# Half of the second-half weight sums of down made ahead in attention, with moved loads and reordered ends, in a one-core encoder layer

## What is computed

```python
def forgetting_attention(h, w_in, b_f, g_q, g_k, w_out):
    proj = jnp.einsum('bsd,de->bse', h, w_in)
    q = rmsnorm(q, g_q)
    k = rmsnorm(k, g_k)
    log_f = jax.nn.log_sigmoid((f_logit + b_f).astype(jnp.float32))
    c = jnp.cumsum(log_f, axis=1).transpose(0, 2, 1)
    ...
        s = jnp.einsum('bqhd,bkhd->bhqk', qb, k).astype(jnp.float32) * scale
        s = s + (cb[..., :, None] - c[..., None, :])
        p = jax.nn.softmax(s, axis=-1).astype(v.dtype)
    ...
    return jnp.einsum('bsd,de->bse', o, w_out)

def swiglu(h, w_gu, w_down):
    gu = jnp.einsum('bsd,df->bsf', h, w_gu)
    gate, up = gu[..., :D_FF], gu[..., D_FF:]
    return jnp.einsum('bsf,fd->bsd', jax.nn.silu(gate) * up, w_down)
```

## Time and profile before

| | us |
|---|---|
| median of 3 runs (2125.92 to 2126.33) | 2126.15 |
| the profiled execution | 2126.24 |
| its span, first to last instruction | 2124.3 |
| PE busy | 2109.8 (99%) |
| DVE busy | 1524.6 (72%) |
| ACT busy | 943.3 (44%) |
| POOL busy | 192.8 (9%) |

### The profile page before, as it was taken

One profiled execution on the slowest core, in us unless ns is written; L12 is line 12 of the kernel. 1 busy time (PEld: TensorE's weight loads), 2 busy tenths in 40 slices (PEclk: granted clock), 3 DMA queues, 4 the chain that ended last, 5 costly groups with the idle time before them and its releaser, 6 DMA issues.

```text
span 2124.3 us, 28271 instructions
## 1 busy us (share of the span) xinstructions
PE 2109.8 (99%) x10402; PEld 1846.7 (87%) x10402; DVE 1524.6 (72%) x2106; ACT 943.3 (44%) x1279; POOL 192.8 (9%) x355
## 2 busy tenths in 40 slices
PE   9999999999999999999999999999999999999998
PEld 8999999999998888888888888888888788887886
DVE  4565566565455435888888888987988977969978
ACT  6333333333344325444444444444544554554533
POOL 0332332233221000000000000000000000000000
PEclk9999999999999999999999999999999999999999
DMA  6465656665243334666666666666666887867866
GB/s 187 118 190 185 211 186 189 198 197 178 80 123 139 119 119 144 203 206 194 226 220 198 219 211 212 209 222 212 198 232 226 276 277 240 266 220 259 266 193 208
DMA packets 269052, 422.45 MB, mean 199 GB/s; under 512 B 17010, under 2 KB 116372, under 8 KB 265636
## 3 DMA queue, kind: packets, MB, share of 16 engines
q1 hardware_dynamic: 248336, 354.77, 52.9%
q10 hardware_dynamic: 20628, 66.49, 8.8%
HBM read 369.52 MB, written 51.68 MB: 198 GB/s over the span
## 4 chain that ended last, share of the span: by engine, by line
PE 96%; DVE 2%; DMA 1%; issue 0%; SPq 0%; ACTq 0%; DVEq 0%
PE gemm L596 11%; PE gemm L597 11%; PE gemm L598 11%; PE gemm L800 11%; PE gemm L802 11%; PE gemm L801 11%; PE aux L800 8%; PE aux L802 8%; PE aux L801 8%; PE aux L597 1%; PE aux L598 1%; PE aux L596 1%; PE aux L851 1%; PE aux L650 1%; DVE f_lo L1475 1%; PE aux L622 0%
## 5 line engine op out<-in xcount | busy, mean ns | idle before, releaser
L1475 DVE TENSOR_TENSOR f_lo<-f_raw,f_hi 128x1536 fp32r<-128x1536 f32 (+1 forms) x230 | 455.0, 1983 | 73.6 <-ACT f_hi L1133 41.3
L596 PE MATMUL gemm<-w_hi,act_t 128*128 128x384 f32 (+2 forms) x1280 | 450.7, 352 | 0.0
L597 PE MATMUL gemm<-w_lo,act_t 128*128 128x384 f32 (+2 forms) x1280 | 443.9, 347 | 0.0
L598 PE MATMUL gemm<-w_hi,act_t 128*128 128x384 f32 (+2 forms) x1280 | 443.9, 347 | 0.0
L800 PE MATMUL gemm<-f_hi,a_form 128*128 128x512 f32 x1056 | 411.1, 389 | 0.0
L802 PE MATMUL gemm<-f_hi,a_form 128*128 128x512 f32 x1056 | 411.0, 389 | 0.0
L801 PE MATMUL gemm<-f_lo,a_form 128*128 128x512 f32 x1056 | 410.8, 389 | 0.0
L800 PE MATMUL aux<-f_hi,a_form 128*128 128x512 f32 x792 | 311.8, 394 | 3.1 <-DVE f_lo L1475 2.5
L802 PE MATMUL aux<-f_hi,a_form 128*128 128x512 f32 x792 | 308.4, 389 | 0.0
L801 PE MATMUL aux<-f_lo,a_form 128*128 128x512 f32 x792 | 308.4, 389 | 0.0
L1089 ACT ACTIVATE f_hi<-f_raw 128x1536 fp32r<-128x1536 f32 x132 | 196.3, 1487 | 214.6 <-DMA f_raw<-in_ffn_w_gate_up 78.7
(11 more groups left out here) (188 smaller groups left out, 2255.3 us busy)
## 6 DMA issues: line engine op xcount, KB each, us to landing
f_raw<-in_ffn_w_gate_up SPq DMA_DIRECT2D x264, 512.0 KB, 4.2
w_raw<-in_fox_w_in SPq DMA_DIRECT2D x189, 256.0 KB, 3.5
f_raw<-in_ffn_w_down SPq DMA_DIRECT2D x88, 512.0 KB, 4.6
f_raw<-in_ffn_w_gate_up SPq DMA_DIRECT2D x88, 256.0 KB, 4.0
f_raw<-t_scratch SPq DMA_DIRECT2D x44, 512.0 KB, 4.8
w_raw<-in_fox_w_out SPq DMA_DIRECT2D x16, 1024.0 KB, 5.1
pre_w<-in_ffn_w_down ACTq DMA_DIRECT2D x22, 512.0 KB, 5.3
pre_rows<-in_ffn_w_down ACTq DMA_DIRECT2D x22, 512.0 KB, 7.1
```

The costliest lines, as they stand in the source:

```text
L596: mm(out, a_hi, b_hi, start=first, stop=False)
L597: mm(out, a_hi, b_lo, start=False, stop=False)
L598: return mm(out, a_lo, b_hi, start=False, stop=last)
L1475: v.tensor_tensor(f_lo[:, n % 4, 0:3 + g], f_raw[:, n % 4, 0:3 + g], f32(f_hi[:, n % 3, 0:3 + g]), ALU.subtract).then_inc(f_lo_done, 1)
```

## The change

Three sets of sums a head in place of two. The third is the second column half (`col = u // 2 * CW`) of the even steps; it is loaded in slot 10 into the first set's buffer, once the first set's store has landed, added on DVE in slot 13 and stored in slot 15. Rounds 12, 14 and 16 (odd `r - R_DOWN`) thereby find ready sums for 4, 4 and 3 of their 8, 7 and 7 steps, and skip L1520 to L1527 for these. Most entries of the `LOADS` tables move by one or two units. At the start the transposes of the second half of x's first column block move behind PE's first six real matmuls, 8 filling matmuls become 6, and ACT issues three small loads (`load_wf`) after its first weight split. At the end the last two stores of block 3 go to ACT's queue.

```diff
+    def early_sums(r, j):
+        if r < R_DOWN:
+            return False
+        return (r - R_DOWN) % 2 == 0 or (FIRST[(r - R_DOWN) // 2] + j) % 2 == 0
...
-    dram_t = nc.dram_tensor("t_scratch", (PRE_END, 2, P, 4, CW), F32, kind="Internal").ap()
+    dram_t = nc.dram_tensor("t_scratch", (PRE_END, 3, P, 4, CW), F32, kind="Internal").ap()
...
-        LOADS_1 = [(0, 0, 0, 4), (0, 1, 1, 6), (0, 2, 4, 10), (0, 3, 7, 13), (0, 4, 8, 14), (0, 5, 8, 14), (0, 6, 11, 17), (1, 0, 9, 14), (1, 1, 12, 18), (1, 2, 13, 19), (1, 3, 14, 19), (1, 4, 14, 20), (1, 5, 16, 20), (1, 6, 17, 23)]
+        LOADS_1 = [(0, 0, 0, 5), (0, 1, 1, 6), (0, 2, 5, 11), (0, 3, 7, 12), (0, 4, 10, 14), (0, 5, 8, 13), (0, 6, 11, 17), (1, 0, 9, 14), (1, 1, 12, 18), (1, 2, 13, 20), (1, 3, 14, 18), (1, 4, 14, 19), (1, 5, 14, 19), (1, 6, 17, 26)]
...
-                    made = dram_t[PRE_FIRST + step // 2, step % 2]
+                    made = dram_t[PRE_FIRST + step // 2, step % 2 if (r - R_DOWN) % 2 == 0 else 2]
...
-            sp.wait_ge(c22_out[0], 1)
-            sp.dma_start(y_cols[3][:, 2], rows[:, 3, 2]).then_inc(y_stored, 16)
...
-            sp.wait_ge(c22_out[1], 1)
-            sp.dma_start(y_cols[3][:, 3], rows[:, 3, 3]).then_inc(y_stored, 16)
...
                         rows_slot(G[t], 0, 0, t, True, False, width, ks=(2 * half, 2 * half + 1))
+                        if half == 0 and t == 0:
+                            pe.wait_ge(x_ld[0], 16)
+                            transpose_rows(0, 0, (2, 3))
...
-            keep_warm(5)
-            pe.wait_ge(x_ld[0], 16)
-            transpose_rows(0, 0, (2, 3))
-            keep_warm(3)
+            keep_warm(6)
...
             def load_blocks(h, u):
-                act.wait_ge(pre_stored[u], 16 * (h - PRE_FIRST) + 16)
-                src = w_down_v[bass.ds(h - PRE_FIRST, 1), u].rearrange("o p r c x -> (o p) r c x")
+                if u == 1:
+                    act.wait_ge(pre_stored[1], 16 * (h - PRE_FIRST) + 16)
+                else:
+                    act.wait_ge(pre_stored[0], 32 * (h - PRE_FIRST) + 8 * u + 16)
+                src = w_down_v[bass.ds(h - PRE_FIRST, 1), u % 2].rearrange("o p r c x -> (o p) r c x")
+                col = u // 2 * CW
...
                     if sums and s in (8, 13):
                         store_sums(h, {8: 0, 13: 1}[s])
+                    if sums and s == 10:
+                        load_blocks(h, 2)
...
                     if s >= 13:
                         evac(h, s - 13)
+                    if sums and s == 15:
+                        store_sums(h, 2)
...
+            for t in range(2):
+                act.wait_ge(c22_out[t], 1)
+                act.dma_start(y_cols[3][:, 2 + t], rows[:, 3, 2 + t]).then_inc(y_stored, 16)
...
                     if s >= 13:
                         evac(h, s - 13)
+                    if sums and s == 13:
+                        pre_sums(h, 2)
                     if s >= 14:
                         normalise_qk(h, s - 14)
...
-                sums = n + 2 < NU and UNITS[n + 2][1] == 1 and not summed_early(UNITS[n + 2][0])
+                sums = n + 2 < NU and UNITS[n + 2][1] == 1 and not summed_early(n + 2)
```

More of the change, by code:

```diff
@@ L85, in encoder_layer @@
         his += 1 + g_
-        ts += g_ and (r_ < R_DOWN or (r_ - R_DOWN) % 2 == 1)
+        ts += g_ and not early_sums(r_, j_)
         HI_COUNT.append(his)
@@ L332, in encoder_layer, with summed_early @@
         assert len(SPLIT_NTH) == 2 * NSTEP
-        def summed_early(r):
-            return r >= R_DOWN and (r - R_DOWN) % 2 == 0
+        def summed_early(n):
+            return early_sums(UNITS[n][0], UNITS[n][2])
         w_down_v = w_down.rearrange("(g r i p) (c x) -> g i p r c x", r=2, i=2, p=P, c=2)
@@ L432, in _ @@
                     sp.dma_start(f_raw[:, s, 2], src[:, 1, 1, col:col + CW]).then_inc(f_ld[s], 16)
-                elif not summed_early(r):
+                elif not summed_early(n):
                     for half in range(2):
@@ L438, in _ @@
                     if r == R_DOWN and j == 0:
-                        for b in range(2):
-                            sp.wait_ge(pre_stored[b], 16 + 8 * NSTEP)
-                    made = dram_t[PRE_FIRST + step // 2, step % 2]
+                        sp.wait_ge(pre_stored[0], 16 + 16 * NSTEP)
+                        sp.wait_ge(pre_stored[1], 16 + 8 * NSTEP)
+                    made = dram_t[PRE_FIRST + step // 2, step % 2 if (r - R_DOWN) % 2 == 0 else 2]
                     for half in range(2):
@@ L913, in _ @@
             act.dma_start(b_f_all[:], b_f.broadcast_to((P, NH))).then_inc(bf_ld, 16)
-            for kg in range(1, KG):
-                load_wf(kg)
             def transposed_hi(n, kg, i):
@@ L976, in load_blocks @@
             def load_blocks(h, u):
[L977 to L978 removed]
+                if u == 1:
[4 more added lines that the diff above has]
+                col = u // 2 * CW
                 for r in range(2):
[L980 removed]
+                    act.dma_start(pre[u % 2][:, 2 * r:2 * r + 2], src[:, r, :, col:col + CW])\
+                        .then_inc(pre_ld[u % 2], 16)
             def store_sums(h, u):
[L983 removed]
+                act.wait_ge(pre_step, 9 * (h - PRE_FIRST) + 3 * u + 3)
                 dst = dram_t[bass.ds(h, 1), u].rearrange("o p f x -> (o p) f x")
[L985 removed]
+                act.dma_start(dst, pre[u % 2][:]).then_inc(pre_stored[u % 2], 16)
             def in_chunk(h, second=False, last=False, sums=False):
@@ L1034, in _ @@
                 split_hi(0, 0, half, in_proj=True, first=True)
+                if half == 0:
+                    for kg in range(1, KG):
+                        load_wf(kg)
             for kg in range(KG):
@@ L1060, in form_read @@
                 act.wait_ge(xform_tr, 2 * q + 1)
+                if q == 0:
+                    act.wait_ge(pre_stored[0], 16 + 16 * NSTEP)
                 if 0 < q < 6:
@@ L1090, in weights_hi @@
                 else:
-                    if not summed_early(r):
+                    if not summed_early(n):
                         act.wait_ge(t_step, 3 * T_COUNT[n] + 1)
@@ L1130, in weights_hi_rest @@
             def weights_hi_rest(n):
-                if not summed_early(UNITS[n][0]):
+                if not summed_early(n):
                     act.wait_ge(t_step, 3 * T_COUNT[n] + 3)
@@ L1375, in pre_sums @@
             def pre_sums(h, u):
-                f = pre[u]
-                dve.wait_ge(pre_ld[u], 32 * (h - PRE_FIRST) + 32)
+                f = pre[u % 2]
+                if u == 1:
+                    dve.wait_ge(pre_ld[1], 32 * (h - PRE_FIRST) + 32)
+                else:
+                    dve.wait_ge(pre_ld[0], 64 * (h - PRE_FIRST) + 16 * u + 32)
                 on_its_own(dve)
                 v.tensor_tensor(f[:, 0:2], f[:, 0:2], f[:, 1:4:2], ALU.add).then_inc(pre_step, 1)
-                dve.wait_ge(pre_step, 6 * (h - PRE_FIRST) + 3 * u + 1)
+                dve.wait_ge(pre_step, 9 * (h - PRE_FIRST) + 3 * u + 1)
                 on_its_own(dve)
                 v.tensor_tensor(f[:, 3], f[:, 0], f[:, 3], ALU.add).then_inc(pre_step, 1)
-                dve.wait_ge(pre_step, 6 * (h - PRE_FIRST) + 3 * u + 2)
+                dve.wait_ge(pre_step, 9 * (h - PRE_FIRST) + 3 * u + 2)
                 on_its_own(dve)
```

4 lines of the change are left out of this document (2 added, 2 removed).

## The result

The changed kernel takes 2129.45 us (median of 13 runs, 2128.24 to 2131.74), the kernel before 2125.92 us (13 runs, 2122.05 to 2127.51). The ratio is 1.0017 with a 95% interval of 1.0010 to 1.0024: 3.5 us more, just under the 0.2% that the prediction called "slower". Forecast were 5.3 us more.

What follows compares the result with a forecast made beforehand. PE, busy 2109.8 of 2124.3 us, was taken to bound the kernel. Profiled 2126.24 + 10.7 (attention) - 4.9 (down) - 0.1 (start) - 0.4 (end) = 2131.5, 2131.4 as median; range for 8 in 10: 2120.3 to 2136.0.

Steps and rivals of the forecast that it cites:

- The chain in attention: Attention, heads 2 to 12: third set's additions behind tile 0's readout delay tile 3's norm; 0.97 us a head, 10.7 us.
- rival A: Attention hides the third set, PE never waits for tile 3's norm: 2120.7 us, ends 2120 and 2124; chance 0.2.
- the stop of 0.2 us at tile 1: Attention: tile 1's norm ends at 334.27, PE transposes at 334.24 and must load first, so PE is 0.2 us late.
- The bounds of 0.2 to 0.3 us: Attention's low end: POOL's step at 0.30 us and additions without 0.29 us of waits leave 0.2 to 0.3 a head.
- rival B: Attention dearer: third loads land later than 8.6 us, or POOL holds up the additions; 15.1 us, 2135.8 total; chance 0.12.
- Nothing to spare: Attention: third set's loads at worst land at 327.3, when DVE wants them at 327.30, so they cost zero.
- Down: Of 5.5 us lost in down, 4.9 come back; ends 2.2 (only backlog goes) and 5.5.
- round 10 and 11's stops: Down: round 10's 1.2 us go as one form is moved out of the way; round 11's 0.6 hang on it.
- Round 14's: Down: DVE backlog stops from 1943 on, 1.6 us, vanish; the 1.1 us stop at 1939.12 goes by an earlier form.
- Round 12's: Down: 0.7 us of stops go because one form is moved out of the way, as in round 10.
- Rival C: Down: the moved forms bring nothing and only backlog goes, 2134.1 us; chance 0.1.
- The ends: Start: 0.1 us won (0 to 0.4); end, last store on ACT: 0.4 us won (0 to 0.5).

## Why the prediction held, point by point

**What bounds.** Right: PE's stops moved the time, and in single profiles the stretch of half clock.

**The chain in attention.** The mechanism, its place and its threshold were right, and the rival A falls for this place: the period is 40.0 us and PE waits eleven times for tile 3's norm. The size was 10.7 us predicted against 8.3 measured, 0.97 against 0.76 a head. This head runs 2.40 us later than the one of the earlier trace rows, so the predicted times are shifted by that:

| step | predicted | measured |
|---|---|---|
| tile 1's norm starts | 336.19 | 336.06 |
| tile 2's norm starts | 338.0 | 337.85 |
| weights' low part behind tile 3's readout | 339.1 | 338.93 |
| tile 3's norm ends | 342.1 | 341.92 |
| PE goes on | 342.25 | 341.98 |

0.17 us were lost over the chain, most of it by the first step, and 0.1 by the last: I added 0.15 us for PE's load behind the norm, and the row shows 0.06 (0.05 come back, since the next matmul follows a little later behind the stop). For the same reason the stop of 0.2 us at tile 1 isn't there: its norm ends at 336.57, and PE goes on at 336.63, on time. That term of the sum was mis-sized, the rest holds. The bounds of 0.2 to 0.3 us and of rival B were not reached.

**POOL beside DVE.** POOL's first two steps for tile 0 lie beside the additions and the third beside the weights' low part behind them (the first three rows); those of tile 2 lie beside none of these:

```profile
329.95 1.05 POOL L523 TENSOR_SCALAR mean_qk<-ss_qk,rms_sq 128x2 f32<-128x2 f32 x1 [14.40 <-DVE ss_qk L1327]
331.19 1.10 POOL L527 TENSOR_TENSOR inv_qk<-mean_qk,neg_half 128x2 f32<-128x2 f32 x1 [0.18 <-POOL mean_qk L523]
332.51 1.07 POOL L531 TENSOR_SCALAR fac_qk<-inv_qk,rms_x 128x2 f32<-128x2 f32 x1 [0.22 <-POOL inv_qk L527]
...
336.12 0.30 POOL L523 TENSOR_SCALAR mean_qk<-ss_qk,rms_sq 128x2 f32<-128x2 f32 x1
336.61 0.71 POOL L527 TENSOR_TENSOR inv_qk<-mean_qk,neg_half 128x2 f32<-128x2 f32 x1 [0.18 <-POOL mean_qk L523]
337.52 0.29 POOL L531 TENSOR_SCALAR fac_qk<-inv_qk,rms_x 128x2 f32<-128x2 f32 x1 [0.20 <-POOL inv_qk L527]
```

POOL takes 3.2 us of work there; in the kernel before, with only its first step beside such an instruction (the weights' low part), it was 0.83 + 0.72 + 0.29 = 1.84, and eleven times the difference are the 15 us of the page. Tile 0's factor comes 1.4 us later for it, at 333.58, but tile 1's readout ends only at 334.10, so nothing waits for that. The additions themselves take 1.22, 0.69 and 0.69 us, and start 1.36 and 0.84 us after each other, exactly as the second set's with no POOL beside them (319.22, 320.58 and 321.42 in the trace of before). So the half of rival B by which POOL holds up the additions is refuted. The Trainium skill, page "SBUF — State Buffer", section "SBUF: two separate sides", has the two shut each other out whichever comes first. The trace agrees for POOL, which waits; a wait of DVE for POOL no row here shows, though the third addition (331.86) starts while POOL's second step (331.19 to 332.29) runs.

**The loads.** Right that they cost nothing: they landed in time in every head, with and without the move. "Nothing to spare" was too tight, since in the changed kernel the later one was there 0.75 to 2.5 us ahead of the additions. The other half of rival B is refuted.

**Down.** 4.9 us were predicted. 5.1 is the difference of the two profiles, 3.7 that of the profiles' means; the profile of before was the worst of its kind. By the medians it is 4.2 to 4.6: the kernel with the third set moved, which has both parts and no cost in attention, is 4.5 and 4.9 us below before in its two runs, 0.3 of it at the end. The steps: round 10 and 11's stops were given to the tables, and the table above bears it out. Round 14's were split into a stop for the tables and backlog for the sums, and both are needed there. Round 12's were given to the tables, and belong more to the sums. Round 16's 0.3 were to vanish with the sums; 0.3 are lost at unit 261 in the changed kernel too. What failed is another step: the stops of one execution were taken as fixed amounts. The one at unit 227 was 1.1 us before, and 0.2 or nothing in four other kernels with the old tables; the one at 173 was 0.5 to 2.5. Rival C, that the moved forms bring nothing, falls: alone they bring 4.1 us, and 1.9 to 2.8 in the three pairs.

**The ends.** 0.5 us predicted, 0.3 measured. The start gives nothing: PE's first real matmul stands at 10.87 us in place of 12.20, and the eight transposes behind it take the gain again. As predicted, ACT issues the last store less than 0.1 us after the last sum (0.04).

**The slow clock.** I took 0 for the stretch at 65 us and named 1.6 us as its bound; the profile of after lacks it and gains 0.9 us net of the stop at 81.6. That, and a profile of before that lost more in down than others of its kind, is why the two profiled executions are only 2.0 us apart.

**The sum.** Forecast were 10.7 - 4.9 - 0.5 = 5.3 us. Measured are 8.3 less 4.5 to 4.9 for down and the end, 3.4 to 3.8, and 3.5 for the change itself; so the account closes within its noise. By the profiles' means it would be 8.3 - 3.7 - 0.3 = 4.3. The 2.4 us too much in attention are the larger error. In down and at the ends the gain was taken some 0.5 to 0.9 too large, which made up for a part of it; that the errors had opposite signs was luck. The chances were less good than the range: "slower by over 0.2%" had 0.57, "within" had 0.24, and 1.0017 lies just within.

## What to carry to other kernels

An engine that idles two fifths of the time (DVE in attention, 59% busy from 125 to 560 us) still has places where it is the link between three others. Ahead of putting work into its gaps, follow the chain from that point to the next wait of the bound engine: 1.8 us behind a readout cost nothing here, 2.8 cost 0.76 a head, and 5.6 cost 3.56, while the same 2.8 us ahead of the readout, where the trace shows an idle time of 2.84, were free. And before work is taken off an engine to cure its stops, see which of them begin with a late transfer: moving single loads gave about as much here as dropping eleven sets of sums.

## What was not expected of the hardware

- The slow stretch after the forget gates' small matmuls comes in three of twelve profiles, and no edit tells which. It costs 1.6 us each time it comes, but 0.6 to 1.1 of it are not seen a head later, since PE, later by it, doesn't wait for the probabilities near 82 us, where it waits 0.3 to 0.8 us in the other nine. In the kernel with two more instructions, stops of some 1.8 us at a head's start were followed by a clock of half speed in five of eleven heads (0.66 to 0.68 on average over the 5 us behind them), while the other six, the stops of 0.5 to 0.6 us in the changed kernel and one of 2.35 us in round 10 (old tables) were not.
- Executions of the kernel before lay between 2122.05 and 2131.86 us. In gate and up, which no edit touched, the stops at late transfers differ by up to 3.4 us between profiles. One profile of each kernel therefore could not have told the tables from the third set; eleven runs of each could for the tables; for the set they could in one of two pairs. To rank the two they are too few.
